# Decoder block on one core: both parts of the activations pass the high weights in one 512-column matmul (gated output, query down, latent keys, queries)

## The reference

```
first block, layer 0:  x += 0.5*ffn(norm(x)); x += hgrn2(norm(x)); x += 0.5*ffn(norm(x)); x += embedding part
   hgrn2: q, f, i, g = split(h @ w_in); o = gated recurrence over chunks of 64
          o = rmsnorm(o) * sigmoid(g);  return o @ w_out              # gated output, 1024 x 1024
shared:  c_kv, k_r = split(norm(x) @ w_down); kv = rmsnorm(c_kv) @ w_up   # 256 x (16 heads x (128 keys + 128 values))
first block, layer 1:  ffn; x += mla(norm(x)); ffn; embedding part
   mla:   c_q = rmsnorm(h @ w_dq)                                     # query down, 1024 x 512
          q = c_q @ w_uq                                              # 512 x (16 heads x (128 + 64))
          softmax(q_nope k_nope + rope(q_rope) k_rope) v @ w_out
second block: two layers of a gated mixer, with modulation from c @ w_ada
```

## Time and profile before

| what | value |
|---|---|
| time, median of 3 runs | 1497.99 us (1497.97, 1497.99, 1507.82) |
| span of the profiled execution | 1491.3 us |
| the profiled execution's own time | not given apart from its span |
| median less span | 6.7 us |
| PE busy / PEld busy | 1462.6 us (98%) / 1410.3 us (95%) |
| DVE / ACT / POOL busy | 1084.5 us (73%) / 765.5 us (51%) / 170.9 us (11%) |
| granted clock | 1.00 |
| HBM read | 262.44 MB, 177 GB/s over the span |

### The profile page before, as it was taken

The page is one execution under the profiler, slowest core; times in us unless marked ns, Lnnn a source line. Parts: engine busy times, 40 slices in busy tenths (PEclk is TensorE's granted clock), DMA queues, the critical chain, the costliest instruction groups (busy, mean ns, idle before and its releaser), DMA issues.

```text
span 1491.3 us, 31123 instructions
## 1 busy us (share of the span) xinstructions
PE 1462.6 (98%) x12410; PEld 1410.3 (95%) x12410; DVE 1084.5 (73%) x1573; ACT 765.5 (51%) x1154; POOL 170.9 (11%) x218
## 2 busy tenths in 40 slices
PE   7999999999999999999999999999999999999998
PEld 7999999989999999999999899999998996889968
DVE  6886568987897578887667665797558768385692
ACT  6544455465554357554445365554346437454482
POOL 1101013711240110110010000110110100010000
PEclk9999999999999999999999999999999999999999
DMA  7877744326787656777646235787643853047400
GB/s 243 273 253 236 250 142 142 98 73 211 235 277 231 219 150 189 240 255 231 201 150 156 78 99 170 232 284 234 204 161 118 268 156 100 2 146 224 144 1 29
DMA packets 219068, 264.86 MB, mean 178 GB/s; under 512 B 22269, under 2 KB 196317, under 8 KB 218973
## 3 DMA queue, kind: packets, MB, share of 16 engines
q1 hardware_dynamic: 209000, 234.64, 50.4%
q0 software_dynamic: 8960, 27.37, 5.4%
q10 hardware_dynamic: 1013, 1.52, 0.3%
HBM read 262.44 MB, written 1.05 MB: 177 GB/s over the span
## 4 chain that ended last, share of the span: by engine, by line
PE 80%; DVE 11%; ACT 5%; DMA 3%; issue 1%; POOL 0%; SPq 0%; DVEq 0%; ACTq 0%
PE twin L1125 24%; PE twin L1126 23%; PE twin L1127 23%; DVE w_lo L1880 3%; PE twin L1558 1%; PE twin L1800 1%; PE twin L1762 1%; DVE hg_s L2116 1%; ACT w_hi L700 1%; DVE rs L1909 1%; PE twin L1572 1%; PE twin L1570 1%; DMA w_raw<-in_ffn_w_in 1%; DVE hg_f L2098 1%; DVE xl L1886 1%
## 5 line engine op out<-in xcount | busy, mean ns | idle before, releaser
L700 ACT ACTIVATE w_hi<-w_raw 128x1024 fp32r<-128x1024 f32 (+1 forms) x452 | 454.7, 1038 | 420.8 <-PE twin L1127 260.0
L1880 DVE TENSOR_TENSOR w_lo<-w_raw,w_hi 128x1024 fp32r<-128x1024 f32 (+1 forms) x452 | 547.3, 1248 | 147.8 <-ACT w_hi L700 147.5
L1125 PE MATMUL twin<-xh,w_lo 128*128 128x256 f32 x2312 | 651.3, 282 | 1.8 <-DVE xl L2402 0.9
L1126 PE MATMUL twin<-xl,w_hi 128*128 128x256 f32 x2312 | 641.4, 277 | 0.0
L1127 PE MATMUL twin<-xh,w_hi 128*128 128x256 f32 x2312 | 641.3, 277 | 0.0
L1125 PEld LDWEIGHTS twin<-xh,w_lo 128*128 128x128 f32 x2312 | 434.3, 188 | 5.7 <-issue 2.0
L1126 PEld LDWEIGHTS twin<-xl,w_hi 128*128 128x128 f32 x2312 | 434.0, 188 | 1.6 <-issue 1.2
L1127 PEld LDWEIGHTS twin<-xh,w_hi 128*128 128x128 f32 x2312 | 433.7, 188 | 0.2
L1125 PE MATMUL twin<-hh,w_lo 128*128 (+1 forms) x704 | 196.3, 279 | 0.0
L1126 PE MATMUL twin<-hl,w_hi 128*128 (+1 forms) x704 | 196.1, 279 | 0.0
L1127 PE MATMUL twin<-hh,w_hi 128*128 (+1 forms) x704 | 196.1, 279 | 0.0
(11 more groups left out here) (382 smaller groups left out, 1978.8 us busy)
## 6 DMA issues: line engine op xcount, KB each, us to landing
w_raw<-in_ffn_w_in SPq DMA_DIRECT2D x176, 512.0 KB, 4.8
w_raw<-in_ffn_w_out SPq DMA_DIRECT2D x88, 512.0 KB, 4.2
w_raw<-in_w_in SPq DMA_DIRECT2D x52, 512.0 KB, 4.8
mod_raw<-in_w_ada POOLq DMA_DIRECT2D x128, 192.0 KB, 4.4
w_raw<-in_a_w_in SPq DMA_DIRECT2D x32, 512.0 KB, 4.5
w_raw<-in_ple_w_gate SPq DMA_DIRECT2D x16, 512.0 KB, 4.1
w_raw<-in_b_w_out SPq DMA_DIRECT2D x16, 512.0 KB, 3.7
w_raw<-in_w_out SPq DMA_DIRECT2D x16, 512.0 KB, 4.4
```

Of the source, the lines that this page charges most:

```text
L700: A(w_hi[:, c % NSLOT, cols], w_raw[:, c % NRAW, cols], ACT.Copy).then_inc(*did(hi_ready))
L1125: mm(out, lhs[1], rhs[0], start=start, stop=False, skip_group_check=skip)
L1126: mm(out, lhs[0], rhs[1], start=False, stop=False, skip_group_check=skip)
L1880: V.tensor_tensor(w_lo[:, c % NSLOT, cols], w_raw[:, c % NRAW, cols], f32(w_hi[:, c % NSLOT, cols]), ALU.subtract).then_inc(*did(lo_ready))
```

## The change

`joined` takes the place of `three` in four stages. The low and high parts of the activations lie side by side (xx, ckx, cqx, and a view of hg_o), so that w_hi is loaded once and one matmul of 512 columns makes xl·w_hi in columns 0 to 255 of a bank and xh·w_hi in columns 256 to 511. xh·w_lo goes into columns 0 to 255. So an output tile fills a whole bank, and the halves are added when it is read: ScalarE copies the low half out of PSUM and VectorE adds the high half (query down, keys, queries), or VectorE adds both, one after the other (gated output). xh and xl are interleaved for all stages that use them. The banks: gated output 4, 5 for even chunks and 6, 7 for odd ones; query down 4, 5 and 6, 7, with the modulation's sums in bank 2; keys in banks 0 to 3 for every u, one head a bank, values in 4, 5 or 6, 7; queries in 0, 1 or 4, 5, rotary halves in 2 or 3, swaps in 6 or 7.

```diff
@@ -192,8 +192,8 @@
...
-    ckh = fixed("ckh", [P, 2, T], F32R)
-    ckl = fixed("ckl", [P, 2, T], F32R)
+    ckx = fixed("ckx", [P, 2, 2, T], F32R)
+    ckl, ckh = ckx[:, :, 0, :], ckx[:, :, 1, :]
...
@@ -206,8 +206,8 @@
...
-    xh = fixed("xh", [P, KD, T], F32R)
-    xl = fixed("xl", [P, KD, T], F32R)
+    xx = fixed("xx", [P, KD, 2, T], F32R)
+    xl, xh = xx[:, :, 0, :], xx[:, :, 1, :]
...
@@ -257,9 +257,8 @@
...
-    hg_oh = place("hg_oh", [P, KD, T], F32R)
-    place, _ = at_offset(region + 3 * KD * T * 4)
-    hg_ol = place("hg_ol", [P, KD, T], F32R)
+    hg_o = place("hg_o", [P, 3, KD, T], F32R)
+    hg_ol, hg_oh = hg_o[:, 0], hg_o[:, 2]
...
@@ -287,8 +286,8 @@
...
-    cqh = place("cqh", [P, 4, T], F32R)
-    cql = place("cql", [P, 4, T], F32R)
+    cqx = place("cqx", [P, 4, 2, T], F32R)
+    cql, cqh = cqx[:, :, 0, :], cqx[:, :, 1, :]
...
@@ -952,22 +951,34 @@
...
+            act.wait_ge(*when(("dq", j)))
+            A(cq[:, 2 * j:2 * j + 2, :], twin[2 + j][:, :, 0:T], ACT.Copy).then_inc(*did(act_steps, ("cqlow", j)))
...
+            for n in range(2):
+                act.wait_ge(*when(("k", u, n)))
+                A(kn[:, 4 * u + 2 * n:4 * u + 2 * n + 2, :], twin[n][:, :, 0:T], ACT.Copy).then_inc(*did(act_steps, ("knlow", u, n)))
...
-                A(vb[:, b, 512 * u:512 * u + 512], bank[4 * (u % 2) + 2 + b][:, :], ACT.Copy).then_inc(*did(act_steps, ("vb", u, b)))
+                A(vb[:, b, 512 * u:512 * u + 512], bank[4 + 2 * (u % 2) + b][:, :], ACT.Copy).then_inc(*did(act_steps, ("vb", u, b)))
...
-                A(std2[:, :], bank[4][:, 0:T], ACT.Sqrt, bias=eps[:, :], scale=1.0 / 512).then_inc(*did(act_steps, "cqstd"))
+                A(std2[:, :], bank[6][:, 0:T], ACT.Sqrt, bias=eps[:, :], scale=1.0 / 512).then_inc(*did(act_steps, "cqstd"))
...
-        for u in range(8 - AHEAD):
-            hi(first["uq"] + u + AHEAD)
+        for u in range(8):
+            if u < 8 - AHEAD:
+                hi(first["uq"] + u + AHEAD)
+            act.wait_ge(*when(("qnope", u)))
+            A(qn[:, 2 * u:2 * u + 2, :], twin[2 * (u % 2)][:, :, 0:T], ACT.Copy, scale=SCALE_B).then_inc(*did(act_steps, ("qnlow", u)))
+            act.wait_ge(*when(("chunk", first["uq"] + u)))
+            if u >= 2:
+                act.wait_ge(*when(("qr", u - 2)))
+            A(qraw[:, u % 2, :], bank[2 + u % 2][:, 0:T], ACT.Copy, scale=SCALE_B).then_inc(*did(act_steps, ("qrlow", u)))
...
@@ -1125,6 +1136,31 @@
...
+
+        def joined(b, w, x, start, stop):
+
+
+
+            mm(b[:, 0:T], w[1], x[:, 1, :], start=start, stop=False, skip_group_check=True)
+            return mm(b[:, :], w[0], x, start=False, stop=stop, skip_group_check=True)
+
+        def columns_joined(c, b, x, waits, name, mods_of=None):
+
+
+            w = split(c, (KD, 256))
+            for n in range(2):
+                take(b + n)
+            for i in range(2 * KD):
+                n, k = (i // KD, i % KD) if waits is None else (i % 2, i // 2)
+                if n == 0 and k % 4 == 0:
+                    pe.wait_ge(lo_ready, 2 * c + 1 + k // 4)
+                if waits is not None and n == 0:
+                    pe.wait_ge(*when(waits(k)))
+                last = joined(bank[b + n], [a[:, k, n * P:(n + 1) * P] for a in w], x[:, k], k == 0, k == KD - 1)
+                if mods_of is not None and i < 2 * KD - 1:
+                    mod_sums(*mods_of, i, 2 * KD - 1)
+            last.then_inc(*did(pe_groups, name))
+            at[("chunk", c)] = at[name]
...
@@ -1418,8 +1454,10 @@
...
-            columns(first["aout"] + j, 4 + j, (hg_oh, hg_ol), (lambda k: ("ol", k // 2)) if j == 0 else None, ("aout", j))
-            release[4 + j] = ("x", 2, j)
+            columns_joined(first["aout"] + j, 4 + 2 * (j % 2), hg_o[:, 0::2].rearrange("p a k n -> p k a n"),
+                           (lambda k: ("ol", k // 2)) if j == 0 else None, ("aout", j))
+            for n in range(2):
+                release[4 + 2 * (j % 2) + n] = ("x", 2, j)
...
@@ -1484,8 +1522,9 @@
...
-            columns(first["dq"] + j, 4 + j, xs, xwait(7) if j == 0 else None, ("dq", j), mods_of=(2, 7) if j else None)
-            release[4 + j] = ("cq", j)
+            columns_joined(first["dq"] + j, 4 + 2 * j, xx, xwait(7) if j == 0 else None, ("dq", j), mods_of=(2, 2) if j else None)
+            for n in range(2):
+                release[4 + 2 * j + n] = ("cqa", j)
...
@@ -1493,33 +1532,32 @@
...
-            b0 = 4 * (u % 2)
+            b0 = 4 + 2 * (u % 2)
...
-                take(b0 + n)
...
+                    take(h)
...
-                        last = three(bank[b0 + n][:, (h % 2) * T:(h % 2 + 1) * T], [a[:, k, h * 256:h * 256 + P] for a in w],
-                                     [ckh[:, k, :], ckl[:, k, :]], k == 0, k == 1)
+                        last = joined(bank[h], [a[:, k, h * 256:h * 256 + P] for a in w], ckx[:, k], k == 0, k == 1)
+                    release[h] = ("kn", u, n)
...
-                release[b0 + n] = ("kn", u, n)
...
-                take(b0 + 2 + t)
+                take(b0 + t)
...
-                    last = three(bank[b0 + 2 + t][:, :], [a[:, k, t * P:(t + 1) * P] for a in (ckh, ckl)], vw, k == 0, k == 1)
+                    last = three(bank[b0 + t][:, :], [a[:, k, t * P:(t + 1) * P] for a in (ckh, ckl)], vw, k == 0, k == 1)
...
-                release[b0 + 2 + t] = ("vb", u, t)
+                release[b0 + t] = ("vb", u, t)
...
-                take(4)
+                take(6)
...
-                    last = mm(bank[4][:, 0:T], ones[:, :], sq[:, k, :], start=(k == 0), stop=(k == 3))
+                    last = mm(bank[6][:, 0:T], ones[:, :], sq[:, k, :], start=(k == 0), stop=(k == 3))
...
-                release[4] = "cqstd"
+                release[6] = "cqstd"
...
-            b = 4 + u % 2
+            b = 6 + u % 2
...
@@ -1529,21 +1567,21 @@
...
-            b0 = 2 * (u % 2)
-            take(b0)
+            b0 = 4 * (u % 2)
...
+                take(b0 + h)
...
-                    last = three(bank[b0][:, h * T:(h + 1) * T], [a[:, k, h * NOPE:(h + 1) * NOPE] for a in w],
-                                 [cqh[:, k, :], cql[:, k, :]], k == 0, k == 3)
+                    last = joined(bank[b0 + h], [a[:, k, h * NOPE:(h + 1) * NOPE] for a in w], cqx[:, k], k == 0, k == 3)
+                release[b0 + h] = ("qn", u)
...
-            release[b0] = ("qn", u)
-            take(b0 + 1)
+            b = 2 + u % 2
+            take(b)
...
-                last = three(bank[b0 + 1][:, 0:T], [a[:, k, 2 * NOPE:] for a in w], [cqh[:, k, :], cql[:, k, :]], k == 0, k == 3)
+                last = joined(bank[b], [a[:, k, 2 * NOPE:] for a in w], cqx[:, k], k == 0, k == 3)
...
-            release[b0 + 1] = ("qraw", u)
+            release[b] = ("qraw", u)
...
@@ -2172,7 +2210,10 @@
...
-            V.tensor_tensor(X[:, 2 * j:2 * j + 2, :], X[:, 2 * j:2 * j + 2, :], two(bank[4 + j][:, :]), ALU.add).then_inc(*did(dve_steps, ("x", 2, j)))
+            x = X[:, 2 * j:2 * j + 2, :]
+            V.tensor_tensor(x, x, twin[2 + j % 2][:, :, 0:T], ALU.add).then_inc(*did(dve_steps))
+            dve.wait_ge(*did.last)
+            V.tensor_tensor(x, x, twin[2 + j % 2][:, :, T:2 * T], ALU.add).then_inc(*did(dve_steps, ("x", 2, j)))
...
@@ -2289,13 +2330,19 @@
...
-                modulation(2, 7)
-            V.tensor_tensor(cq[:, 2 * j:2 * j + 2, :], two(bank[4 + j][:, :]), rep(rs[:, :], 2), ALU.mult).then_inc(*did(dve_steps, ("cq", j)))
+                modulation(2, 2)
+            pair_ = slice(2 * j, 2 * j + 2)
+            dve.wait_ge(*when(("cqlow", j)))
+            V.tensor_tensor(cq[:, pair_, :], cq[:, pair_, :], twin[2 + j][:, :, T:2 * T], ALU.add).then_inc(*did(dve_steps, ("cqa", j)))
+            dve.wait_ge(*did.last)
+            V.tensor_tensor(cq[:, pair_, :], cq[:, pair_, :], rep(rs[:, :], 2), ALU.mult).then_inc(*did(dve_steps, ("cq", j)))
...
-                V.tensor_copy(kn[:, 4 * u + 2 * n:4 * u + 2 * n + 2, :], two(bank[4 * (u % 2) + n][:, :])).then_inc(*did(dve_steps, ("kn", u, n)))
+                keys = kn[:, 4 * u + 2 * n:4 * u + 2 * n + 2, :]
+                dve.wait_ge(*when(("knlow", u, n)))
+                V.tensor_tensor(keys, keys, twin[n][:, :, T:2 * T], ALU.add).then_inc(*did(dve_steps, ("kn", u, n)))
...
@@ -2310,7 +2357,7 @@
...
-            V.tensor_tensor(qr_t[:, 1, :], bank[4 + u % 2][:, 0:T], sin[:, :], ALU.mult).then_inc(*did(dve_steps, ("q_sin", u)))
+            V.tensor_tensor(qr_t[:, 1, :], bank[6 + u % 2][:, 0:T], sin[:, :], ALU.mult).then_inc(*did(dve_steps, ("q_sin", u)))
...
@@ -2319,11 +2366,14 @@
...
-            V.tensor_scalar(qn[:, 2 * u:2 * u + 2, :], two(bank[2 * (u % 2)][:, :]), SCALE_B, None, ALU.mult).then_inc(*did(dve_steps, ("qn", u)))
+            queries = qn[:, 2 * u:2 * u + 2, :]
+            dve.wait_ge(*when(("qnlow", u)))
+            V.scalar_tensor_tensor(queries, twin[2 * (u % 2)][:, :, T:2 * T], SCALE_B, queries, ALU.mult, ALU.add).then_inc(*did(dve_steps, ("qn", u)))
...
```

(3 more changed lines are left out.)

## The result

The changed kernel took 1519.03 us (1512.87 to 1521.69, 4 runs) beside 1497.98 (1497.21 to 1507.82, 4 runs) for before: ratio 1.0112, 95% interval 1.0077 to 1.0146. Run again on another chip: 1512.20 us (1505.88 to 1520.19, 10 runs) beside 1502.41 (33 runs), ratio 1.0062 (1.0036 to 1.0088). It is slower, by 10 us by the larger sample; the two intervals just overlap.

The account below looks back on a forecast made before the run. TensorE, busy 98% of the span, was taken as the bound. Gated output 4.6, query down and keys 4.3, queries 0.4, less 0.2 gained by pairs, gave +9.1 us: 1507.1 us, range 1500 to 1515.

Parts of the forecast that it names:

- the two stops it named: TensorE idle 4.6 us before the third gated-output chunk (VectorE's X add) and 3.3 us before the third latent-key head (sums read).
- slower by more: Outcome of the whole kernel slower by more than about 1%, which needs 1513 us; chance 0.14.
- within 1%: Outcome of the whole kernel within about 1% (15 us) of before; chance 0.84.
- The pair: A 256-column and a 512-column matmul per product: 0.3505 us in place of 0.3525; bounds gain 0.0125 and no gain.
- Gated output, +4.6: Chunk 2 waits from 343.00 to 347.6 for VectorE's two adds of chunk 0 into X; bounds 0.9 and 6.5 us.
- Query down and keys, +4.3: Latent stage: 3.4 us by group 1's start, stop at the sums included, plus 0.9 before group 2; bounds 1.5 and 6.0.
- the wait before group 2: Latent keys: TensorE ready at 796.8, bank 0 freed by the key add at 797.7, 0.9 us more.
- The wait before group 1: Latent keys: after the sum over cq ends at 789.8, TensorE waits for the key add ending at 791.2.
- Queries, +0.4: Query projections: only the final swap waits longer, for a ScalarE copy of about 0.4 us; bounds 0 and 0.8.
- Rival 4, the clock falls in a stop: After a stop TensorE restarts at half rate, costing 1 to 3.5 us each: 1508.5 to 1512 us; chance 0.15.
- Rival 3, the spacing changes sides: Matmul stretches flip between 0.113 and 0.117 us: FFN1 long 1513.4 us, chance 0.12; two others short 1502.6, chance 0.10.
- The 6.7 us around the span: Whole kernel: before's median 1497.99 exceeds its profiled span 1491.3 by 6.7 us, added to the forecast span 1500.4.

## Why the prediction was right or wrong

Right in kind: slower, by about 1%, by the two stops it named, with the releasers it named. The median of 1519.03 lies above the range of 1500 to 1515, that of the second batch, 1512.20, inside it. The first ratio, 1.0112, is the case "slower by more" that had a chance of 0.14; the second, 1.0062, is the case "within 1%" that had 0.84. Step by step:

- **The pair.** Forecast 0.3505 us, gain 0.002; measured 0.353 in the gated output and in the queries. That is no gain against three matmuls at the long spacing, the bound "0.3525, no gain", and a loss of 0.013 against three at the short one, which no bound had. By the Trainium skill (TensorE: Matmul & The Clock Gate, "Back-to-back issue gap") it would have been 0.325; no trace here shows that.
- **Gated output, +4.6.** Measured +3.7. The banks came free where forecast (347.6; TensorE went on at 347.46). TensorE came later than 343.00, at about 343.86, because the trace of after is 0.86 us late at the gated output's start, a low-clock stretch at 315 us included, while the transfers were not. Against the 22.65 or 22.66 us of four other traces with three matmuls there it is +4.4: a shorter stop than forecast, plus the pair's loss. That the total comes nearer to 4.6 so is luck.
- **Query down and keys, +4.3.** The stop was 3.7 us for 3.3, the wait before group 2 0.89 for 0.9. The wait before group 1 did not come: 802.48 stands 1.54 us behind the sum at 800.94, back to back. TensorE, at half rate, was too late to wait. In its place stands the clock, 2.9 us. Without these 2.9 the stretch to the scores is +3.8 us, against a forecast 4.3 + 0.4 - 0.2 = 4.5 with the queries.
- **Queries, +0.4.** 0.5 more at the last swap (0.69 against 0.17), as argued.
- **Rival 4, the clock falls in a stop, chance 0.15.** This is the step that failed: "Against it: nothing slowed after the 1.06 us stop at 787.79". A stop of 1 us is no evidence on stops of 3 to 4. Nine traces here have stops of 2.9 to 4.6 us in mid-program, 12 in all, and 10 bring a low-clock stretch (the two that aren't are the 3.4 and 3.5 us before chunk 2 in the changed kernel's two traces). It should have been part of the forecast, +2 to +4 us; over 10 runs the clock's share was +3.8. Its price was summed wrongly too: 1 to 3.5 us at each of two stops on 1507.1 is 1509.1 to 1514.1, not "1508.5 to 1512". The Trainium skill's rule (TensorE: Matmul & The Clock Gate, "What's actually happening") is that an idle array falls back to half rate. The traces agree with it at 10 of these 12 stops, and the prediction gave it too little weight.
- **Rival 3, the spacing changes sides.** It does, without any change. In the changed kernel FFN1's first half went long, for 3.7 us in place of the 6.3 that were priced for both its halves. Traces of one kernel differ by up to 5 us in a half. It widened the scatter, and made the trace of before a favourable one.
- **The 6.7 us around the span.** "I carry these 6.7 over" was wrong. After's profiled execution took 1.9 us more than its span, and so, I take it, did before's: some 1493.2 us, an execution without a low-clock stretch and faster than all of its runs (1497.21 at the least in the first batch, 1494.32 in all). The gap was not around the span but between executions.

The sum comes out by the rest, within its error: of the 10.9 us by which the second batch's means differ (standard error 1.7), 3.8 are clock and 7.1 are not, and the two stages of the trace, without the clock, give 3.7 + 3.8 = 7.5. That the forecast of 9.1 came near the total is luck: its terms were 1.6 us too long together, while the clock's share of up to 3.8 was missing.

Open: whether the stop before chunk 2 puts FFN1's first half on the long spacing. It stood there in all 5 traces with that stop, and in 3 of the 8 with no stop in the gated output or at FFN1's start: not enough to say. What decides a side was not found.
